# A hybrid decoder step: key pages inside the loop over pairs, value pages in half-page units, page transfers on GpSimd's queue

## What is computed

```python
def token_mix(xn, ...):
    proj = xn @ w_in                       # xn = rmsnorm(x, g_mix)
    q, k, v, z, xbc, dt_raw = jnp.split(proj, ...)
    attn = rmsnorm(attend(q, k, v), g_attn)
    xbc, conv_new = causal_conv(xbc, conv_state, conv_w, conv_b)
    y, ssm_new = ssd_scan(xs, dt, a, b_in, c_in, ssm_state)
    y = (y + d_skip * xs) * silu(z)
    y = _rms(y) * g_ssd                    # by two groups
    return concatenate([attn, y]) @ w_out
```

## Time and profile before

| | us |
|---|---|
| median of 3 runs | 1210.52 (1208.24 to 1213.32) |
| the profiled execution | 1214.61 |
| its span | 1212.5 |
| TensorE (matmul) busy | 1182.2, 98% |
| VectorE busy | 789.5, 65% |
| GpSimd busy | 752.8, 62% |
| ScalarE busy | 571.0, 47% |
| mean traffic | 185 GB/s |

### The profile page before, as it was taken

The page is one execution under the profiler, slowest core; times in us unless marked ns, Lnnn a source line. Parts: engine busy times, 40 slices in busy tenths (PEclk is TensorE's granted clock), DMA queues, the critical chain, the costliest instruction groups (busy, mean ns, idle before and its releaser), DMA issues.

```text
span 1212.5 us, 23706 instructions
## 1 busy us (share of the span) xinstructions
PE 1182.2 (98%) x7511; PEld 1025.3 (85%) x7511; DVE 789.5 (65%) x1752; ACT 571.0 (47%) x1287; POOL 752.8 (62%) x622
## 2 busy tenths in 40 slices
PE   7999999999999999999999999999999999999997
PEld 5877777645988899999999999999888888888876
DVE  4669787756139999500589999994454456666544
ACT  3222323342425555556455554444555555555545
POOL 0049341004836599998766666666767688789755
PEclk9999999999989999999999999999999999999999
DMA  5555575487645376665554554454666688778653
GB/s 210 153 194 177 171 269 157 125 304 239 188 140 157 90 219 189 189 184 169 180 146 140 140 144 144 140 141 140 185 188 190 191 281 284 240 261 295 202 155 110
DMA packets 99863, 224.88 MB, mean 185 GB/s; under 512 B 11682, under 2 KB 12306, under 8 KB 99274
## 3 DMA queue, kind: packets, MB, share of 16 engines
q1 hardware_dynamic: 96762, 214.52, 57.6%
q0 software_dynamic: 2304, 8.39, 2.0%
q10 hardware_dynamic: 720, 1.01, 0.2%
HBM read 215.61 MB, written 8.19 MB: 185 GB/s over the span
## 4 chain that ended last, share of the span: by engine, by line
PE 69%; issue 1%; DVE 0%; POOL 0%; ACT 0%; DVEq 0%; POOLq 0%; ACTq 0%
PE bank L1533 30%; PE bank L1563 29%; PE bank L1543 5%; PE bank L1486 2%; PE bank L1498 1%; PE bank L1510 1%; PE bank L1583 0%; PE bank L1600 0%; POOL hl L1426 0%; DVE acts L1959 0%; PE bank L1591 0%; ACT acts L1769 0%; POOL hl L1411 0%; PE bank L1618 0%; PE bank L1576 0%
## 5 line engine op out<-in xcount | busy, mean ns | idle before, releaser
L1411 POOL TENSOR_TENSOR hl<-ring,hl 128x512 fp32r<-128x512 f32 x448 | 586.2, 1319 | 184.4 <-ACT hl L1649 177.3
L1649 ACT CAST hl<-ring 128x512 fp32r<-128x512 f32 x512 | 317.1, 620 | 290.2 <-PE bank L1563 159.6
L1533 PE MATMUL bank<-split,hl 128*128 128x256 f32 x3072 | 378.5, 282 | 0.4 <-ACT hl L1649 0.3
L1533 PEld LDWEIGHTS bank<-split,hl 128*128 128x128 f32 x3072 | 366.3, 188 | 0.8 <-issue 0.5
L1563 PE MATMUL bank<-hl,split 128*128 128x512 f32 x1524 | 353.6, 394 | 0.0
L1563 PEld LDWEIGHTS bank<-hl,split 128*128 128x128 f32 x1524 | 286.0, 188 | 67.7 <-issue 0.9
L483 PE MATMUL pj<-xn,ring 128*128 128x264 f32 x704 | 167.4, 394 | 2.1 <-DMA ring<-in_w_ring 2.1
L483 PEld LDWEIGHTS pj<-xn,ring 128*128 128x128 f32 x704 | 133.3, 193 | 28.3 <-issue 4.0
L1929 DVE TENSOR_TENSOR split<-acts,split 128x256 fp32r<-128x256 f32 x128 | 130.3, 1042 | 37.9 <-ACT split L1745 34.2
L1936 DVE TENSOR_TENSOR hl<-ring,hl 128x512 fp32r<-128x512 f32 x64 | 45.3, 707 | 118.2 <-ACT hl L1649 118.2
L459 POOL TENSOR_TENSOR wo<-ring,wo 128x512 fp32r<-128x512 f32 x32 | 46.9, 1473 | 93.4 <-ACT wo L863 93.3
(11 more groups left out here) (334 smaller groups left out, 1156.5 us busy)
## 6 DMA issues: line engine op xcount, KB each, us to landing
ring<-in_uv SPq DMA_DIRECT2D x256, 256.0 KB, 2.8
ring<-in_v_rows SPq DMA_DIRECT2D x256, 256.0 KB, 3.1
ring<-in_w_ring SPq DMA_DIRECT2D x76, 512.0 KB, 3.7
room<-in_cache_k SPq DMA_DIRECT2D x16, 512.0 KB, 5.9
room<-in_cache_v SPq DMA_DIRECT2D x16, 512.0 KB, 4.7
hs<-in_state_ssm SPq DMA_DIRECT2D x8, 512.0 KB, 4.8
out_ssm_s<-hs SPq DMA_DIRECT2D x8, 512.0 KB, 5.2
acts<-x_rows SPq DMA_DIRECT2D x8, 512.0 KB, 4.3
```

The source lines that it names most:

```text
L1411: nc.gpsimd.tensor_tensor(hl[:, r % HL, 1], raw[:, r], hl[:, r % HL, 0].bitcast(F32), ALU.subtract).then_inc(lo_done, 1)
L1533: mm = nc.tensor.matmul(out, hl[:, r % HL, m, k * P:(k + 1) * P], split[:, x, kk, 0:TP], start=(kk == 0 and n == 0), stop=(kk == KD - 1 an ...
L1649: nc.scalar.copy(hl[:, r % HL, 0], raw[:, r]).then_inc(hi_done, 1)
```

## The change

- *First tiles.* `xg` = x times g_mix (in `mix`'s memory) is the moving operand of tiles 0 and 1 and of dt; VectorE multiplies the result by 1/rms when it empties the bank (`evict_early`), and ScalarE only passes the count on. 18 products of the small tile `pick` stand ahead of tile 0. VectorE adds the squares, so one product of ones is left. `xn` is made in two halves, for tile 2 on.
- *Queues.* The stores of `acs` and `bc_rows` and the broadcast go from SP's to ScalarE's queue, ahead of copies 8 and 10. The convolution state and the masks are issued after the squares. The transposes that stood after tiles 4 and 6 stand after 6 and 7.
- *Key pages.* A key unit is one pair of feature blocks of four samples: 8 transfers of 128 KB. The 8 units are multiplied in pairs 2, 4 and 6 (two each) and in pair 7 (two), into `swb` and `bcp`, four samples at partitions 0, 32, 64 and 96. ScalarE spreads q into `q6w` per pair. VectorE clears the banks first, and takes one maximum per four samples in pair 7; the exponentials are two instructions for all eight samples.
- *Value pages.* A value unit is half the width of one page of four samples: 4 transfers of 256 KB, 4 products of 16 rows over 512 columns. The new position's share of the softmax is joined at the end (`sample_rates`, `sample_factors`, `spread_rates`).
- *GpSimd* issues all 96 page transfers: three key units before the first state update, keys 3 to 6 after updates 3 to 6, keys 7 and the values after the last.

Cut to the core:

```diff
+        xg = mix[:, 0:KD]
...
-        pages = part(room, 0, NS, D)
+        key_slots = part(room, 0, SLOTS, SIDE, NPG, 2, P)
+        val_slots = part(room, 0, SLOTS, SIDE, D // 2)
...
+        q6w = part(rstd[:].rearrange("p a n -> p (a n)"), 0, 2, NB, WIN)
+        pt6, p6 = part(flath, 0, NQ, NPG, P), part(flath, NQ * NPG * P, NQ, PAST)
+        v6 = part(flath, NB * P, NQ, D)
+        val_homes = [val_slots[:, s] for s in range(SLOTS)] + [part(flath, NB * P, SIDE, D // 2)]
+        V_HOME = (2, 3, 0, 1, 2, 0, 1, 2)
...
-                def page(n):
-
-                    if n >= NS:
-                        sp.wait_ge(page_used, n - NS + 1)
-                    b, g = n // NPG % NB, n % NPG
-                    at = sp.value_load(ptab[0:1, b * NPG + g:b * NPG + g + 1], min_val=0, max_val=t["n_pool"] - 1)
-                    cache = t["cache_k"] if n < NB * NPG else t["cache_v"]
-                    sp.dma_start(pages[:, n % NS], cache[bass.ds(at, 1)].rearrange("a p n -> p (a n)")
-                                 ).then_inc(page_full[n % NS], 16)
...
-                    if i == 10:
-                        sp.wait_ge(bc_copied, 1)
-                        sp.dma_start(t["bc_rows"].rearrange("a b n -> b a n"), brow).then_inc(bc_kept, 16)
-                    if i == CONV_CH - 1:
-                        sp.wait_ge(bc_kept, 16)
-                        sp.wait_ge(dd_done, 1)
-                        sp.dma_start(wide, t["bc_rows"].rearrange("(o a) b n -> o (a b n)", o=1).broadcast_to([P, 2 * GROUPS * NB * P])
-                                     ).then_inc(bc_in, 16)
-                    if i == 9:
-                        sp.wait_ge(acs_ready, 1)
-                        sp.dma_start(t["acs_rows"], acs[:]).then_inc(acs_kept, 16)
                 sp.wait_ge(acs_kept, 16)
...
+                pool.wait_ge(normed, 2)
+                pool.wait_ge(early_out, 2)
+                nc.gpsimd.memset(q6w.rearrange("p a b n -> p (a b n)"), 0.0).then_inc(zeroed, 1)
+
+                def page_of(b, g):
+
+                    return pool.value_load(ptab[0:1, b * NPG + g:b * NPG + g + 1], min_val=0, max_val=t["n_pool"] - 1)
+
+                def keys(u, samples=range(SIDE)):
+
+                    cc, q, s = u // NQ, u % NQ, u % SLOTS
+                    if u >= SLOTS:
+                        pool.wait_ge(unit_used, u - SLOTS + 1)
+                    for j in samples:
+                        for g in range(NPG):
+                            at = page_of(q * SIDE + j, g)
+                            pool.dma_start(key_slots[:, s, j, g].rearrange("p c n -> p (c n)"),
+                                         t["cache_k"][bass.ds(at, 1)].rearrange("a p n -> p (a n)")[:, 2 * cc * P:2 * (cc + 1) * P]
+                                         ).then_inc(key_full[s], 16)
+
+                def values(n):
+
+                    q, m, g = n // (2 * NPG), n // NPG % 2, n % NPG
+                    if V_HOME[n] == SLOTS:
+                        pool.wait_ge(ys_done, KD - 1)
+                        for s in (1, 2):
+                            pool.wait_ge(hs_out[s], 16 * (KD // HS))
+                    else:
+                        pool.wait_ge(unit_used, (KU - 2, 0, KU - 1, KU, KU + 1, KU + 3, KU + 4, KU + 5)[n])
+                    for j in range(SIDE):
+                        at = page_of(q * SIDE + j, g)
+                        pool.dma_start(val_homes[V_HOME[n]][:, j],
+                                     t["cache_v"][bass.ds(at, 1)].rearrange("a p n -> p (a n)")[:, m * 4 * P:(m + 1) * 4 * P]
+                                     ).then_inc(val_full[V_HOME[n]], 16)
+
+                pool.wait_ge(ptab_in, 16)
+                pool.wait_ge(bc_kept, 16)
+                pool.wait_ge(silu_done, CONV_CH)
+                pool.wait_ge(silus_done, 2)
+                for u in range(SLOTS):
+                    keys(u)
...
+                    if 3 <= c < KD - 1:
+                        keys(c)
+                keys(KU - 1)
+                for n in range(VU):
+                    values(n)
...
+                        if i == 0:
+                            pe.wait_ge(xg_done, k + 1)
+                        if i == 2 and k % 4 == 0:
+                            pe.wait_ge(normed, k // 4 + 1)
...
+                pe.wait_ge(picked, 2)
+                flat = pick[:].rearrange("p c h -> p (c h)")
+                for n in range(18):
+                    nc.tensor.matmul(yb[:, 0:P], flat, flat, start=True, stop=True)
+                tile(0)
+                pe.wait_ge(cst_in, 16)
+                pe.wait_ge(pre1, 1)
+                nc.tensor.matmul(hd[0][:, 0:NT], ones, sq[:, 0], start=True, stop=True).then_inc(summed, 1)
+                pe.wait_ge(wdt_in, 16)
+                for k in range(KD):
+                    mm = nc.tensor.matmul(hd[1][0:NH, 0:NT], wdt[:, k], xg[:, k], start=(k == 0), stop=(k == KD - 1))
+                mm.then_inc(dt_ready, 1)
 
...
+                def key_unit(u):
+
+                    cc, q, s = u // NQ, u % NQ, u % SLOTS
+                    if u == 0:
+                        pe.wait_ge(cleared6, 3)
+                    pe.wait_ge(q_spread, 4 * cc + 4)
+                    pe.wait_ge(key_full[s], 16 * SIDE * NPG * (u // SLOTS + 1))
+                    for x in range(2):
+                        c = 2 * cc + x
+                        for j in range(SIDE):
+                            mm = nc.tensor.matmul(part((swb, bcp)[q][j * SPAN:j * SPAN + NH], 0, NPG, P),
+                                                  q6w[:, x, q * SIDE + j, NH - 2 - 2 * c:2 * NH - 2 - 2 * c],
+                                                  key_slots[:, s, j, :, x], start=(c == 0), stop=(c == KD - 1))
+                    mm.then_inc(unit_used, 1)
+
                 for c in range(KD):
...
+                    if c and c % 2 == 0:
+                        key_unit(c - 2)
+                        key_unit(c - 1)
...
+                    if c == KD - 1:
+                        key_unit(KU - 2)
+                        key_unit(KU - 1)
...
+                def value_unit(n):
+
+                    q, m, g = n // (2 * NPG), n // NPG % 2, n % NPG
+                    if n == 0:
+                        pe.wait_ge(pts_ready, 1)
+                    pe.wait_ge(val_full[V_HOME[n]], 16 * SIDE * (V_HOME[:n].count(V_HOME[n]) + 1))
+                    for j in range(SIDE):
+                        mm = nc.tensor.matmul(o6_bank[q][m][j * SPAN:j * SPAN + NH], pt6[:, q, g, j * SPAN:j * SPAN + NH],
+                                              val_homes[V_HOME[n]][:, j], start=(g == 0), stop=(g == NPG - 1))
+                    mm.then_inc(unit_used, 1)
+
+                pe.wait_ge(qk6_ready, 1)
                 pe.wait_ge(picked, 2)
+                pe.wait_ge(pj_copied, N_IN)
                 for c in range(KD):
-                    mm = nc.tensor.matmul(bcp[0:NH, 0:NB], pick[:, c], qk6[:, c], start=(c == 0), stop=(c == KD - 1))
+                    for j in range(SIDE):
+                        mm = nc.tensor.matmul(pj[1][j * SPAN:j * SPAN + NH, 0:NQ], pick[:, c], qk6[:, c, j::SIDE],
+                                              start=(c == 0), stop=(c == KD - 1))
                 mm.then_inc(own_ready, 1)
-                pe.wait_ge(dds_done, 1)
-                key_pages(0, 1)
+                turn_sample_probs()
+                turn_probs(KD - 1)
+                pe.wait_ge(h1_done, KD)
+                value_unit(0)
+                value_unit(1)
+                attend(KD - 1)
+                value_unit(2)
+                value_unit(3)
                 pe.wait_ge(y_done, KD)
-                key_pages(1, 2)
-                turn_probs(KD - 1)
-                key_pages(2, 4)
-                attend(KD - 1)
-
-                def turn_sample_probs(first, end):
-
-                    for b in range(first, end):
-                        pe.wait_ge(p6_ready, b + 1)
-                        for g in range(NPG):
-                            mm = nc.tensor.transpose(hd[1][:, (g * NB + b) * NH:(g * NB + b + 1) * NH], p6[:, b, g * P:(g + 1) * P],
-                                                     cst[0:NH, C_ID:C_ID + NH])
-                    return mm
-
...
+                    if i == 8:
+                        act.wait_ge(acs_ready, 1)
+                        act.dma_start(t["acs_rows"], acs[:]).then_inc(acs_kept, 16)
+                        act.wait_ge(bc_ready, 1)
+                        nc.scalar.copy(brow.rearrange("b a n -> b (a n)"), hd[0][0:NB]).then_inc(bc_copied, 1)
+                        act.wait_ge(bc_copied, 1)
+                        act.dma_start(t["bc_rows"].rearrange("a b n -> b a n"), brow).then_inc(bc_kept, 16)
+                    if i == 10:
+                        act.wait_ge(bc_kept, 16)
+                        act.wait_ge(dd_done, 1)
+                        act.dma_start(wide, t["bc_rows"].rearrange("(o a) b n -> o (a b n)", o=1).broadcast_to([P, 2 * GROUPS * NB * P])
...
```

(28 more changed lines are left out.)

319 lines of the change are left out of this document (137 added, 182 removed).

## The result

The changed kernel takes 1229.41 us (1228.22 to 1233.01, four runs), the kernel before 1211.82 beside it: ratio 1.016 (95% interval 1.0129 to 1.0191), so 1.6% slower. The forecast was 1200.9, faster, with a range of 1186 to 1222. The time lies outside it, on the other side, 5.6 us under my slow rival (b), though the price X of a transfer, on which that rival hung, was forecast right.

The account below looks back on a forecast made before the run. TensorE bounds the kernel, with VectorE close behind in the pair loop. 12.3 + 24.0 + 1.5 - 7.2 - 21.0 = 9.6 us gained, so 1200.9 us from a median of 1210.52; range 1186 to 1222 (8 in 10).

Parts of the forecast that it names:

- rival (b): GpSimd's page transfers: read and issue in series, 1.96 us each; burst stall and late values give 1235; chance 0.17.
- X: Price of one GpSimd page transfer, taken as 1.10 us, bounds 0.86 to 1.96.
- What bounds: TensorE sets the sample stretch and nearly fills the pair loop; from 296.13 us the change touches little.
- 1 and 2, opening and convolution: Tile 2 starts 6.4 us sooner, convolution waits and clock falls go: 12.3 us gained by the end of pair 0.
- rival (e): Opening: weights come no earlier than 9.7 us, costing 2 us, within the range; chance 0.08 together with rival (d).
- 3, the burst: Before the loop: 24 key transfers delay state update 0; VectorE stalls 19.1 us, plus 1.9 clock fall: 21.0 lost.
- Later units hide: 8.2 + 8 x 1.1 = 17 us of GpSimd in a pair of 20.: Pair loop: a state update and 8 transfers fit on GpSimd within a pair, so later key units cost nothing.
- rival (d): VectorE holds GpSimd up: transfers wait for its operations, the burst meets about 2.5 us; 1203.5; chance 0.08 with rival (e).
- 4, key products: Pairs 2, 4, 6 and 7: packed key products cost 7.2 us, 1.5 credited for waits TensorE already had.
- 5, the sample stretch: Pair 7's scores to first output product: page work leaves TensorE, VectorE's chain is late next; 25.9 us saved.
- rival (c): Sample stretch pays half: the walk leaves out waits, or values come late; 12 us less, 1213; chance 0.10.
- less a fall of the clock in so much waiting, 1.9: Sample stretch: one clock fall from TensorE's waiting costs 1.9 us, leaving 24.0 of the 25.9 saved.

Follow-up runs that it names:

- tail_order: Changed kernel with the sums' products ahead of value units 4 to 7 on TensorE and sample factors ahead of the sums' read on VectorE; 1222.1 us (1.0088).
- sync_even_busy: sync_even_more with 48 idle products on TensorE, spread over all its waits of the sample stretch; 1189.0 us (0.9818).
- spread_keys: Changed kernel with the first three key units behind state updates 0, 1 and 2, not ahead of the loop; 1211.23 us (0.9992).
- one_gap: Changed kernel with one GpSimd wait, for its own decay products, moved ahead of the input products, making a pause between two batches; 1229.2 us.
- state_first: Changed kernel with each state update from 4 on ahead of the 8 key transfers in GpSimd's queue, the burst kept; 1224.6 us (1.0111).
- sync_queue: Changed kernel with all 96 page transfers issued by SyncE, the keys 8 to 16 behind a pair's weights; 1204.3 us (0.9932).
- keys_on_sync: Changed kernel with the 64 key transfers issued by SyncE and the 32 value transfers still by GpSimd; 1200.9 us (0.9894).
- half_reads: Changed kernel with one page number read for every two key transfers, so every second page's keys are wrong; 1220.6 us (1.0071).
- sync_even_more: sync_queue with both moves of tail_order and every key unit cut into groups of four, one behind a weight tile each; 1194.5 us (0.9863).

## Why the prediction was wrong, point by point

**What bounds.** Right for the loop: where VectorE or GpSimd stood still, TensorE did. Wrong for what comes after 296 us. I wrote that the change touches little there; it lost 8.4 us there.

**1 and 2, opening and convolution: 12.3 forecast, 10.5 measured.** Tile 2 starts at 21.43, not 19.2, since tile 0 waits 1.26 us for its weights and starts at 9.90 and not at 8.1: rival (e), 2 us. The end of pair 0 scatters by as much: it is at 79.3 in after and at 77.5 to 80.6 in the other runs with this opening. The two falls of the clock went (1.00 in 0.00:65.95).

**3, the burst: 21.0 forecast, 21.6 measured.** X was to be 1.10 and is 1.15, the mechanism, the place and the engine that stands still are as told. That the sizes agree so closely is in part luck: the burst began at 68.4 and not at 64.8, VectorE asked at 82.2 and not at 80.3, the update took 7.5 and not 8.2 us. GpSimd's 64 key issues took 0.536 to 0.737 us, and 38 of them overlap an operation of VectorE. The rule of the Trainium skill ("SBUF — State Buffer", section "SBUF: two separate sides") for an issue that is locked out beside a copy is not seen in them, and the 1249 us estimated from it didn't come. VectorE's copies beside them read PSUM banks, though, so a copy from SBUF to SBUF wasn't among what they met.

**The failed step in 3: "Later units hide: 8.2 + 8 x 1.1 = 17 us of GpSimd in a pair of 20."** That sum is right and the conclusion is wrong. It counts GpSimd's time and not what the transfers do to the start of the state update behind them. They pushed updates 4 and 6 into the softmax of pairs 3 and 5, at a transfer's end, where VectorE is shut out for two batches: 5.3 + 4.1 us. My rival (d) had the two engines holding each other up the other way round, GpSimd by VectorE, and only 2.5 us of it.

**4, key products: 5.7 net forecast (7.2 less 1.5), 3.6 measured.** Four at a time as read from the earlier trace rows; a unit is about 0.9 us. Part of it lies under waits that were there.

**5, the sample stretch: 25.9 forecast up to the first output product, 16.6 measured.** The chain on VectorE is the right chain; the 9.3 us are rival (c), which I had named and given 0.10, and the step that failed is the walk along VectorE's rows alone: 4.0 for the sums behind value unit 4, 3.7 for the sample factors (5.2 for 1.5), and 2.1 because ScalarE's squares come late, behind its copies of an attention output that TensorE multiplies only after two value units:

```profile
267.27 0.76 ACT L814 COPY mix<-hd 64x256 f32<-64x256 f32 x2 [3.08 <-PE hd L541]
270.04 1.26 DVE L1229 TENSOR_TENSOR xn<-xn 128x1056 f32<-128x1056 f32 x1 [4.21 <-ACT xn L904]
```

The rest of the walk came out 0.5 shorter; the kept values' products took 3.4 us, where I had two rounds of 1.85. tail_order gave back 7.6 of the first two's 7.7.

**The failed step in 5: "less a fall of the clock in so much waiting, 1.9".** I priced it as one tile at the old falls of the earlier trace rows. Behind this stretch, in which TensorE was busy 24.9 of 47.2 us, the next 14.5 us were granted 0.62: 14.5 x 0.38 = 5.5 us, an estimate from that row; the whole output projection is 6.2 longer. Only some 2 us of it, the first low stretch, are the fall that I meant, and 1.9 was near. The other 3, the second one behind the small products, had no term. sync_even_busy got the first back (2.5 us in its case) and kept the second.

**No step at all: the seam,** 3.5 us, with its cause open.

The sum with measured sizes, in the spans: -10.5 + 21.6 + 9.4 + 3.6 - 16.6 + 5.5 + 3.5 = 16.5, for 15.9 (the difference is the PEER mixer's 1.3 less, and 0.7 more in the output projection than the clock's estimate). Of the 26.1 us between my -9.6 and that 16.5, 9.4 are the holds, 9.3 the stretch, 3.6 the clock (5.5 less the 1.9 that I had), nearly all of it the second fall, 3.5 the seam, 1.8 the opening and 0.6 the burst, less 2.1 on the key products. Rival (b) gave 1235 for a reason that didn't happen, and it is a coincidence that it came nearer. With the burst right, the sum stood on a tail of 24 us, read from a walk along one engine's rows. I gave its failure one chance in ten and bounded it at 12 us.

## What to carry to other kernels

Work that is moved onto an idle engine has three prices: its length, what it stands in front of, and where it makes the work behind it start. The third needs the other engine's rows in order of time at that place. Right behind an issue GpSimd's batch shut VectorE out, elsewhere it slowed it, and both cost time only where TensorE waited for what VectorE did there: the rotary additions of after were held for 5 us, and TensorE didn't wait for them. A transfer that reads its page number costs its queue about 1.2 us on GpSimd as on SyncE; what decides is that no unit of eight stands ahead of work that somebody waits for, and on SyncE that no more than four stand between two weight tiles. A walk along one engine's rows must follow every wait of the other engines that it passes. When a stretch is freed of TensorE's work, ask what clock the next one begins with, and whether idle products are cheaper than the fall; and read the clock in windows of 1 us before naming one cause for it.

## What the runs showed of the hardware that I had not expected

- VectorE can be shut out by GpSimd for 4.7 to 5.2 us, whatever its operation's size (128x2, 128x128, 128x264). All eight such holds in after and spread_keys begin during a transfer issue of GpSimd, 0.1 to 0.5 us ahead of its first batch, and end at GpSimd's next pause; a pause of 0.17 us is enough (one_gap, 2.48 us). A ninth (2.15 us, spread_keys, 148.51) begins within a batch and ends at the same pause. In state_first (from update 4 on), sync_queue and keys_on_sync, where updates don't start behind an issue, there is none. That the pause ends a hold is tested by one_gap; that the issue begins it is read from these cases, and no run puts a pause between issue and update.
- Beside GpSimd's batches that start otherwise both engines go on, more slowly: the softmax scaling of 128x256 took 0.82 for 0.35 us (one_gap), four operations of 128x128 took 2.80 for 0.87 (state_first). One operation of each engine then takes about equally long (0.82 on VectorE and 0.72 on GpSimd in one_gap, 0.70 and 0.72 in state_first), as if the two took turns; no run tests that.
- Reading a page number takes GpSimd 0.61 us and the issue 0.54, in series (after, half_reads).
- The low clock outlives its cause: behind a stretch at 0.61 with TensorE busy 25 of 42 us, TensorE worked without a pause, and the first 5 us were still granted 0.50, the level of 1.2 GHz (sync_even_more); behind one at 1.00, busy 37.8 of 41.2 us, the first 6 us had 1.00 (sync_even_busy). Eight idle products made no difference.
- It fell without any waiting too: behind 32 records of products with 4 and 16 columns, to 0.50 for 6 us in after and to 0.57 for 4 us in sync_even_busy. 16 records with 8 columns in before had no fall behind them.
- At the end of a part of the program TensorE waits 2.8 us (before), and 6.3 after 96 transfers of GpSimd (after); why is open.
